# A two-layer trunk in float32 on one core: idle products in TensorE's waits, narrow spreads at the recurrence's end, the query norm multiplied into the queries

## The reference, cut to what matters

```python
def rwkv7_time_mix(...):
    ...
    y = wkv7_scan(r_h, heads(decay), k_h, v_h, -kk, kk * heads(a))
    mean = jnp.mean(y, axis=-1, keepdims=True)
    var = jnp.mean(jnp.square(y - mean), axis=-1, keepdims=True)
    y = ((y - mean) * lax.rsqrt(var + RWKV_GN_EPS)).reshape(B, T, C) * ln_w + ln_b
    bonus = jnp.sum(r_h * k_h * r_k, axis=-1, keepdims=True) * v_h
    y = (y + bonus.reshape(B, T, C)) * g
    return y @ w_out, v_raw

def nsa_mix(x, w_in, ...):
    q = rms_norm(proj[..., :NSA_Q_COLS].reshape(B, T, HKV, G, DH), q_norm)
    ...
    s = jnp.einsum('bqhgd,bnhd->bhgqn', qb, k_cmp) * scale - slopes * dist_c
    p_c = masked_softmax(s, dist_c >= 0)
    ...
    s = jnp.einsum('bqhgd,bhqkd->bhgqk', qb, k_sel) * scale - slopes * dist_s
    p_s = masked_softmax(s, dist_s >= 0)
    ...
    o = gb[..., 0:1] * o_c + gb[..., 1:2] * o_s + gb[..., 2:3] * o_w
```

## Time and profile before

| what | us |
|---|---|
| median of 3 runs | 800.62 (800.15 to 806.32) |
| the profiled execution, device time | 797.37 |
| its span, first to last instruction | 795.6 |
| TensorE busy | 744.3 (94%) |
| VectorE busy | 524.5 (66%) |
| ScalarE busy | 384.1 (48%) |
| GpSimd busy | 73.8 (9%) |
| mean granted clock of TensorE | 0.962 |

### The profile page before, as it was taken

One profiled execution on the slowest core, in us unless ns is written; L12 is line 12 of the kernel. 1 busy time (PEld: TensorE's weight loads), 2 busy tenths in 40 slices (PEclk: granted clock), 3 DMA queues, 4 the chain that ended last, 5 costly groups with the idle time before them and its releaser, 6 DMA issues.

```text
span 795.6 us, 18364 instructions
## 1 busy us (share of the span) xinstructions
PE 744.3 (94%) x7720; PEld 698.8 (88%) x7720; DVE 524.5 (66%) x751; ACT 384.1 (48%) x581; POOL 73.8 (9%) x67
## 2 busy tenths in 40 slices
PE   7999997797878999999999998988889999999997
PEld 6988987797747999999999988975569999999997
DVE  3996886757543887875555776676746887764541
ACT  6666543221433544544444443748867454444331
POOL 0000005280130000000000010023320000000000
PEclk9999998999977999999999999988989999999999
DMA  9953330000111599876666544300007566575651
GB/s 290 271 179 109 107 106 2 4 3 7 51 54 54 159 241 245 220 210 213 194 199 187 162 138 122 117 21 2 1 13 227 176 195 206 166 235 190 197 169 53
DMA packets 110893, 109.29 MB, mean 137 GB/s; under 512 B 7120, under 2 KB 109776, under 8 KB 110704
## 3 DMA queue, kind: packets, MB, share of 16 engines
q1 hardware_dynamic: 110832, 108.41, 45.5%
HBM read 107.35 MB, written 1.05 MB: 136 GB/s over the span
## 4 chain that ended last, share of the span: by engine, by line
PE 80%; DVE 10%; ACT 3%; SPq 2%; DMA 1%; issue 1%; POOL 1%; ACTq 0%; DVEq 0%; POOLq 0%
PE ps L449 21%; PE ps L450 20%; PE ps L451 20%; PE ps L664 4%; DVE SB L1972 2%; DMA raw<-in_rwkv_w_in 1%; DVE nmx L1977 1%; ACT SB L1405 1%; DVE Gs L1653 1%; PE ps L958 1%; PE ps L802 1%; PE ps L947 1%; PE ps L563 1%; PE ps L892 1%; DVE wlo L1468 1%
## 5 line engine op out<-in xcount | busy, mean ns | idle before, releaser
L1468 DVE TENSOR_TENSOR wlo<-raw,whi 128x1024 fp32r<-128x1024 f32 x188 | 225.3, 1221 | 88.5 <-ACT whi L1069 86.0
L449 PE MATMUL ps<-xh,whi 128*128 128x256 f32 x896 | 250.9, 280 | 0.5 <-DVE wlo L1468 0.5
L450 PE MATMUL ps<-xl,whi 128*128 128x256 f32 x896 | 247.9, 277 | 0.0
L451 PE MATMUL ps<-xh,wlo 128*128 128x256 f32 x896 | 247.8, 277 | 0.0
L1069 ACT ACTIVATE whi<-raw 128x1024 fp32r<-128x1024 f32 x124 | 130.1, 1058 | 129.2 <-PE ps L451 123.0
L449 PEld LDWEIGHTS ps<-xh,whi 128*128 128x128 f32 x896 | 168.3, 188 | 4.1 <-issue 2.5
L450 PEld LDWEIGHTS ps<-xl,whi 128*128 128x128 f32 x896 | 168.4, 188 | 0.3 <-issue 0.2
L451 PEld LDWEIGHTS ps<-xh,wlo 128*128 128x128 f32 x896 | 168.3, 188 | 0.0
L451 PE MATMUL ps<-hh,wlo 128*128 128x256 f32 x512 | 141.3, 276 | 0.0
L449 PE MATMUL ps<-hh,whi 128*128 128x256 f32 x512 | 141.3, 276 | 0.0
L450 PE MATMUL ps<-hl,whi 128*128 128x256 f32 x512 | 141.3, 276 | 0.0
(11 more groups left out here) (286 smaller groups left out, 1001.3 us busy)
## 6 DMA issues: line engine op xcount, KB each, us to landing
raw<-in_mlp_w SPq DMA_DIRECT2D x128, 512.0 KB, 4.4
raw<-in_rwkv_w_in SPq DMA_DIRECT2D x24, 512.0 KB, 4.9
raw<-in_nsa_w_in SPq DMA_DIRECT2D x20, 512.0 KB, 4.6
raw<-in_rwkv_w_out SPq DMA_DIRECT2D x8, 512.0 KB, 3.5
raw<-in_nsa_w_out SPq DMA_DIRECT2D x8, 512.0 KB, 3.9
cw<-in_nsa_cmp_w SPq DMA_DIRECT2D x4, 512.0 KB, 10.0
cst<-in_consts SPq DMA_DIRECT2D x1, 1047.0 KB, 11.1
xtok<-in_x SPq DMA_DIRECT2D x2, 512.0 KB, 4.6
```

Source lines behind the costliest of these rows:

```text
L449: mm(o, wh, hi[:, kk, :], start=(kk == 0), stop=False)
L450: mm(o, wh, lo[:, kk, :], start=False, stop=False)
L451: last = mm(o, wl, hi[:, kk, :], start=False, stop=(kk == ktiles - 1))
L1468: v.tensor_tensor(wlo[:, slot, :], raw[:, slot, :], whi[:, slot, :].bitcast(f32), ALU.subtract)\
```

## The change

In the inversion four products of `ident` with `chunk` (128x256) go into the PSUM bank of `sq1` before the wait for VectorE, for each stream and pair, and five before the waits in front of `g_products`; nobody reads them. In the recurrence `rsb` is gone: `gn_spread` multiplies the 16 x 64 reciprocals by eight slices of `spread`, one for each 128 features. Gate, bonus and lower part of the last two chunks are on VectorE, with the last chunk's gate multiplied into `YC` before the spread is there; GpSimd does the first two. Idle products (1, 2 and 5) stand in TensorE's queue between the last steps. In the attention the negated reciprocal norm is transposed, copied, spread to 128 features per tile and multiplied into the queries of groups 1 to 3 (`spread_q`, `scale_q`); in these groups slopes are constants, the scale of the exponential is -1 and the third instruction of `soft` is gone. Group 0 stays. Compressed scores, their exponential and gates move by one item, and `ahead(U0["vv"])` moves behind the last `out_lower`.

```diff
                                   start=True, stop=True)
                 last.then_inc(sem(f"inv_pe{s}"), 1)
+            def idle_products(bank, count):
+                for n in range(count):
+                    mm(ps[:, bank, 0:T], cc("ident"), cc("chunk"), start=True, stop=True)
...
                         pe.wait_ge(sem("bkt_dve"), 3)
                     lower_products(s, pair)
                 for s in both:
+                    idle_products(inv_bank(s, pair, "sq1"), 4)
                     dve_did(s, 3)
                     times(s, pair, "sq1", LT, 0)
                 for s in both:
...
                     times(s, pair, "m64b", LT, 0)
+            idle_products(inv_bank(0, NPAIR - 1, "m64a"), 5)
             for s in range(2):
                 pe.wait_ge(sem(f"inv_dve{s}"), NDVE * NPAIR)
             g_products(0)
...
             def gn_spread(c):
                 pe.wait_ge(sem("y_rstd"), c + 1)
-                mm(ps[:, 7, :], spread[0:H, D + FT:], rsb[:, :, :], start=True, stop=True).then_inc(sem("rstd_pe"), 1)
+                for k in range(FT):
+                    last = mm(ps[:, 7, k * C:(k + 1) * C], hspread(k), rst[:, 0:C], start=True, stop=True)
+                last.then_inc(sem("rstd_pe"), 1)
...
                     xs_values(c + 1)
                 if c:
                     gn_spread(c - 1)
+            def keep_warm(count):
+                for n in range(count):
+                    mm(ps[:, 4, 0:T], cc("ident"), cc("chunk"), start=True, stop=True)
             gn_mean(NCH - 1)
+            keep_warm(1)
             gn_var(NCH - 1)
+            keep_warm(2)
             gn_spread(NCH - 1)
+            keep_warm(5)
             pe.wait_ge(sem("yh_ready"), NCH)
-            pe.wait_ge(sem("yl_ready"), NCH - 1)
-            pe.wait_ge(sem("yl_last"), 1)
+            pe.wait_ge(sem("yl_ready"), NCH)
             linear8("o0", yh, yl)
             def mlp_pe(n1, n2, hi, lo, x, i_norm):
...
                               cc("hsel")[:, H - 2:H], start=True, stop=True)
             last.then_inc(sem("nsa_pe"), 1)
             scores(0)
+            pe.wait_ge(sem("nrq_ready"), 1)
+            for q in range(TT):
+                last = nc.tensor.transpose(ps[0:H, 4, q * P:(q + 1) * P], nrq[:, q, :], cc("ident"))
+            last.then_inc(sem("nsa_pe"), 1)
             values(1)
-            pe.wait_ge(sem("q_root"), 1)
+            def spread_q(j):
+                pe.wait_ge(sem("rqT_ready"), 1)
+                if j == 3:
+                    pe.wait_ge(sem("q_scaled"), 1)
+                for k in range(2):
+                    last = mm(ps[:, 7 - 3 * (j == 2), k * T:(k + 1) * T], hspread(2 * j + k), rqT[:, :], start=True, stop=True)
+                last.then_inc(sem("q_spread"), 1)
+            spread_q(1)
             scores(1)
             scores(2)
+            spread_q(2)
+            spread_q(3)
             pe.wait_ge(sem("kcm_r"), 2)
             pe.wait_ge(sem("vblk_r"), 4)
+            pe.wait_ge(sem("q_scaled"), 3)
             for q in range(TT):
                 for k in range(FT):
                     o = q * T + k * 32
...
                 A(rst[:, C:2 * C], ps[0:H, 7, 0:C], ACT.Sqrt, bias=tiny[0:H, 1:2], scale=1.0 / HD).then_inc(sem("y_std"), 1)
             def gn_upper(c):
-                if c < NCH - 1:
+                if c < NCH - 2:
                     act.wait_ge(sem("y_gated"), 2 * c + 2)
                 else:
-                    act.wait_ge(sem("y_last"), 2)
+                    act.wait_ge(sem("y_last"), 2 * (c - NCH + 2) + 2)
...
             act.wait_ge(sem("nsa_pe"), NSA_PE["q_sum"])
             A(nq[:, :, :], ps[:, 3, 0:TT * H].rearrange("p (q h) -> p q h", h=H), ACT.Sqrt, bias=tiny[:, 3:4])\
                 .then_inc(sem("q_root"), 1)
+            act.wait_ge(sem("nsa_pe"), NSA_PE["rq_T"])
+            A(rqT[:, :], ps[0:H, 4, 0:T], ACT.Copy, scale=-1.0).then_inc(sem("rqT_ready"), 1)
             ahead(U0["vv"])
...
                 act.wait_ge(sem("mx_ready"), n + 1)
                 for i in range(4):
                     hd = 4 * j + i
-                    o = A(SB[n % 4][:, i, 0:w], SB[n % 4][:, i, 0:w], ACT.Exp, bias=nmx[:, n % 4, i:i + 1], scale=nrq[:, q, hd:hd + 1],
+                    o = A(SB[n % 4][:, i, 0:w], SB[n % 4][:, i, 0:w], ACT.Exp, bias=nmx[:, n % 4, i:i + 1], scale=nrq[:, q, hd:hd + 1] if j == 0 else -1.0,
                           accum_out=den[:, q, b, hd:hd + 1])
                     step(o)
...
                     values(0)
                 if n == 3:
                     values(1)
-                if n == 1:
+                if n == 2:
                     act.wait_ge(sem("csub"), 1)
                     A(Sc[:, :, :, 0:16], Sc[:, :, :, 0:16], ACT.Exp).then_inc(sem("cexp"), 1)
...
             def gn_rstd(c):
                 dve.wait_ge(sem("y_std"), c + 1)
-                step(v.reciprocal(rst[:, 0:C], rst[:, C:2 * C]))
-                settle()
-                v.tensor_tensor(rsb[:, :, :], rst[:, 0:C].unsqueeze(1).broadcast_to([H, FT, C]),
-                                spread[0:H, D:D + FT].unsqueeze(2).broadcast_to([H, FT, C]), ALU.mult).then_inc(sem("y_rstd"), 1)
+                v.reciprocal(rst[:, 0:C], rst[:, C:2 * C]).then_inc(sem("y_rstd"), 1)
             def gn_scale(c):
...
                 if c:
                     gn_rstd(c - 1)
                 ahead(U0["v"] + 4 + c)
+            def late(c):
+                return YF[c % 2][:, :, :], slice(c * C, (c + 1) * C)
+            def late_lower(c):
+                y, tok = late(c)
+                dve.wait_ge(sem("yh_ready"), c + 1)
+                v.tensor_tensor(yl[:, :, tok], y, yh[:, :, tok].bitcast(f32), ALU.subtract).then_inc(sem("yl_ready"), 1)
             gn_scale(NCH - 2)
-            gn_rstd(NCH - 1)
-            gn_scale(NCH - 1)
-            tok = slice((NCH - 1) * C, T)
-            y = YF[(NCH - 1) % 2][:, :, :]
             dve.wait_ge(sem("gate_folded"), 3)
-            dve.wait_ge(sem("y_scaled"), NCH)
+            y, tok = late(NCH - 2)
+            dve.wait_ge(sem("y_scaled"), NCH - 1)
             v.tensor_tensor(y, y, Gt[:, :, tok], ALU.mult).then_inc(sem("y_last"), 1)
             dve.wait_ge(sem("y_last"), 1)
             v.tensor_tensor(y, y, t11[:, :, tok], ALU.add).then_inc(sem("y_last"), 1)
-            dve.wait_ge(sem("yh_ready"), NCH)
-            v.tensor_tensor(yl[:, :, tok], y, yh[:, :, tok].bitcast(f32), ALU.subtract).then_inc(sem("yl_last"), 1)
+            y, tok = late(NCH - 1)
+            dve.wait_ge(sem("yc"), NCH)
+            dve.wait_ge(sem("yh_ready"), NCH - 2)
+            dve.wait_ge(sem("yl_ready"), NCH - 2)
+            v.tensor_tensor(y, YC[:, :, :], Gt[:, :, tok], ALU.mult).then_inc(sem("yc_gated"), 1)
+            late_lower(NCH - 2)
+            gn_rstd(NCH - 1)
+            dve.wait_ge(sem("rstd_pe"), NCH)
+            dve.wait_ge(sem("yc_gated"), 1)
+            v.tensor_tensor(y, y, ps[:, 7, :].rearrange("p (k n) -> p k n", n=C), ALU.mult).then_inc(sem("y_last"), 1)
+            dve.wait_ge(sem("y_last"), 3)
+            v.tensor_tensor(y, y, t11[:, :, tok], ALU.add).then_inc(sem("y_last"), 1)
+            late_lower(NCH - 1)
             def residual(name, i, gain, x):
...
                 v.scalar_tensor_tensor(kcm[q, :, e, 0:NB], view(ps[q, 5, 0:HKV * 16]), tiny[q, 4:5],
                                        view(gu[q, 1, :]), ALU.mult, ALU.mult).then_inc(sem("kcm_r"), 1)
             dve.wait_ge(sem("q_root"), 1)
-            dve.wait_ge(sem("zeroed"), 7 + H)
-            step(v.tensor_tensor(qsl[:, :, :], nq[:, :, :], slp[:, :].unsqueeze(1).broadcast_to([P, TT, H]), ALU.mult))
-            step(v.tensor_scalar(nq[:, :, :], nq[:, :, :], -1.0, None, ALU.mult))
+            step(v.tensor_scalar(nrq[:, :, :], nq[:, :, :], -1.0, None, ALU.mult))
             settle()
-            step(v.reciprocal(nrq[:, :, :], nq[:, :, :]))
+            v.reciprocal(nrq[:, :, :], nrq[:, :, :]).then_inc(sem("nrq_ready"), 1)
+            dve.wait_ge(sem("zeroed"), 7 + 4)
+            step(v.tensor_tensor(qsl[:, :, :], nq[:, :, 0:4], slp[:, :].unsqueeze(1).broadcast_to([P, TT, 4]), ALU.mult))
             settle()
+            dve.wait_ge(sem("nrq_ready"), 1)
+            def scale_q(j):
+                x = Qn[:, 2 * j:2 * j + 2, :]
+                dve.wait_ge(sem("q_spread"), j)
+                v.tensor_tensor(x, x, ps[:, 7 - 3 * (j == 2), :].rearrange("p (k n) -> p k n", n=T), ALU.mult)\
+                    .then_inc(sem("q_scaled"), 1)
             gv = gat[:, :, :].rearrange("p q (h b) -> p q h b", b=3)
...
             def compressed_scores():
                 dve.wait_ge(sem("nsa_pe"), NSA_PE["sc"])
-                step(v.tensor_tensor(Sc[:, :, :, 0:NB], ps[:, 5, :].rearrange("p (q h n) -> p q h n", q=TT, n=16)[:, :, :, 0:NB],
-                                     nrq[:, :, :].unsqueeze(3).broadcast_to([P, TT, H, NB]), ALU.mult))
+                raw_ = ps[:, 5, :].rearrange("p (q h n) -> p q h n", q=TT, n=16)
```

(21 more changed lines are left out.)

## The result

The median of the changed kernel is 791.75 us (20 executions, 787.63 to 806.44), that of before 798.8 us (20 executions, 796.56 to 809.19). The ratio is 0.9897 with a 95% interval of 0.9872 to 0.9921: about 7 to 8 us less. The forecast was 0.9925 of before and 794.6 us, with a range of 788.5 to 801.0; the time lies in the range and the forecast's ratio just outside the interval, on the side of the smaller gain. The sum came out nearly right, but from terms of which two were wrong by 3 and 4 us, in opposite directions.

What follows compares the result with a forecast made beforehand. The prediction saw TensorE losing time and clock to waits in the inversion, recurrence end and attention. Terms of -1.9, -5.4 and +1.3 us summed to -6.0 us, forecasting 794.6 us, range 788.5 to 801 us.

Steps and rivals of the forecast that it cites:

- Inversion, -1.9 us: Inversion: idle products hold the clock, gaining 3.0 us; the five ahead of `g_products` delay the masks by 1.1 us.
- Rival 1: Inversion and recurrence tail: idle products don't hold the clock, so the kernel slows to 811.5 us; chance 5%.
- Narrow spread, 1.95 us: Recurrence's `gn_spread`: eight 64-column products, 16 records, take 1.95 us in place of one 512-column product of 1.1 us.
- Rivals 3 (0.5 us) and 5 (2.6 us): Group-norm spreads: cheap at 0.5 us each, 788.8 us total, 12%; or loads don't hide, 2.6 us each, 797.2 us, 5%.
- Up to the last mean, -1.5 us: Recurrence before the last mean: +0.2 us twice, and -1.9 us in the item with long `rsb`, where the clock holds.
- Tail, -1.8 us: Recurrence's end, from item 2's scaling to the projection: 10.3 us instead of 12.1, with one VectorE product fewer.
- Clock at `o0`, -2.1 us: Output projection's start: TensorE kept occupied through the tail, so the 2.1 us lost at half clock are gained.
- Into the steady loop, -1.6 us: Attention's start: compressed scores 4 us later, absorbed by TensorE's slack further on; 1.6 us gained into the loop.
- rival 2: Attention: the 4 us delay is not absorbed because ScalarE's first items are late too; +3.8 us there, 797.1 us; 20%.
- Steady loop, -0.9 us: Softmax loop: dropping the third VectorE instruction saves 0.9 us over three groups; immediate operands cost the same.
- The late `ahead`, +2.5 us: Attention loop's end: the last projection waits for `ahead(U0["vv"])`, 1.22 us, behind the last `out_lower`; 2.5 us lost.
- The clock at `o1`, +1.3 us: Last projection's start: 2.2 us of TensorE idling may drop the clock, costing 0 to 2.1 us; 1.3 taken.

Runs made afterwards that it cites:

- no_four: Changed kernel without the four idle products ahead of each first square of the inversion; 797.67 us, one execution.
- best1: Changed kernel without the five idle products, with `ahead(U0["vv"])` back behind softmax item 0 and four idle products ahead of the compressed scores; 789.57 us, 0.9871 of before.
- wide_spread: Changed kernel with the old single wide group-norm product and `rsb` instead of eight narrow products; 792.53 us, 0.9903 of before.
- p_inv: Original kernel with only the inversion's idle products added; 797.19 us, 0.9968 of before.
- p_att: Original kernel with only the attention changed; 798.03 us, 1.0009 of before.
- sc_idle: Changed kernel plus four idle products in the wait ahead of the compressed scores; 788.35 us, 0.9850 of before, five executions.
- no_warm: Changed kernel without the eight idle products at the recurrence's end; 797.62 us, 0.9970 of before.
- no_rec: Changed kernel with the recurrence and its end as in the original; 795.84 us, 0.9953 of before.
- p_inv_rec: Original kernel with the inversion and recurrence changed, attention as before; 800.85 us, 0.9982 of before.
- best1_no_warm: The kernel best1 without the eight idle products at the recurrence's end; 793.31 us, 0.9931 of before.

## Why the prediction came out right, point by point

- **Inversion, -1.9 us: right in every part.** 9.55 us for the 320 records (forecast 9.8), -3.4 us by no_four (-3.0), +1.4 by best1 (+1.1), -2.0 in all. Rival 1, that idle products don't hold the clock, is out.
- **Narrow spread, 1.95 us: right**, 1.99, and 1.92 from its start to that of the next product (234.42 to 236.34). Rivals 3 (0.5 us) and 5 (2.6 us) are out: 16 records, each with its own load on the same 16 rows, start 0.12 us apart. The rule of the Trainium skill that spoke against the spread ("TensorE: Matmul & The Clock Gate", Part 3) would have given 2.6 us by the forecast's estimate; the measurement decides for the overlap.
- **Up to the last mean, -1.5 us: too much.** Measured -0.4, and 0.4 to 0.9 us between kernels with like falls. The step "what follows keeps its clock, another 0.9 us" failed: in after the stretch from 220 to 225 us is at 0.78 and the last mean is at half clock, and its last mean takes 2.05 us with or without `rsb` (wide_spread). The long `rsb` was not what let the clock fall: p_inv and p_att have it and no fall near 220 us, best1 and sc_idle are without it and have one there.
- **Tail, -1.8 us: the sum nearly right (-1.4), one reason missing.** The product saved on VectorE was rightly credited: from the spread's end to `o0` it is 2.94 us instead of 3.85, the larger part of the gain. But the idle products, which I had counted only for the clock at `o0`, carry the tail as well: without them it takes 12.20 us in this form (no_warm), 0.9 more than before's. The terms that the forecast lists for the new tail add up to 8.6 us, and to 9.3 with the scaling ahead of the mean, not to its 10.3; the last 1.0 us is given no source.
- **Clock at `o0`, -2.1 us: right**, about -2.5.
- **Into the steady loop, -1.6 us: wrong, it was +1.6.** The start of the scores was forecast at 521.4 on the old scale, 4.1 us later relative to the query sums; measured 14.49 against 10.29 us, 4.2 later. The term that failed is the next one: I took the clock for unchanged by the new wait of 1.04 us. It was at half through the scores, 7.00 us instead of 3.96, and ate the slack that should have absorbed the delay: the transposes come 33.3 us behind the query sums (535.32 in the lines above) where before had 30.3, though the forecast had them a little earlier. With the clock held (sc_idle) the same delay was absorbed, 38.22 us to item 3 against before's 41.44. The outcome at this place is that of rival 2, but its cause, ScalarE's late first items, is not what the profiles show, and its total for the attention (+3.8 us) did not come.
- **Steady loop, -0.9 us: mis-sized, it was -5.2.** The three groups' worth of the third VectorE instruction is 3 x 0.36 = 1.1 us, near the 0.9. "The immediate operands are the same instructions and cost the same" was false: 3 x 0.96 = 2.9 us. The remaining 1.2 us go with the clock in items 4 to 7, as shown above; why it fell there before and not in after is open. The kind of operand is a mechanism that none of my rivals had; the trace of before has no such instruction with an immediate, and I gave the term no bounds.
- **The late `ahead`, +2.5 us: right**, +2.35, by the wait of 2.11 us that was forecast, on `wlo`. **The clock at `o1`, +1.3 us: 0 in after's profile**, where it stayed at full, but 1.4 us or more in four of the eight profiles with this wait. Between these two the forecast had chosen, and which it is changes with the execution.
- **The sum.** -6.0 forecast; the local terms give -2.0 -0.4 -1.4 -2.5 -1.3 = -7.6 us, the medians -7.05, the lowest runs -8.9. An error of 3.2 us against the change at the loop's start and one of 4.3 in its favour within the loop met in the sum, and so did 1.1 against it ahead of the last mean and 1.3 in its favour at `o1`; that the time fell into the forecast's range was in this part luck. The chances were less well placed than the range: 791.75 us lies under 792.6, for which the forecast had 0.28 against 0.67 for what lies above it up to 808.6.

**What stays open.** What decides the pace. It sets in at breaks of the stream and holds for 30 to 210 us. Behind `o0` the profiles of before, p_att, no_warm and no_rec are without it up to the query sums, the others have it for some stretch; at `o1` only after and no_rec have it. The medians of p_inv_rec, no_warm and wide_spread lie 6 to 9 us above their lowest runs, those of p_inv and p_att 2 to 3 us, which speaks for the recurrence's edit making it more frequent; but after, with that edit, has 4 us, no_rec, without it, 5, and before itself 1.6 to 3.8. Neither the narrow spreads (wide_spread) nor the idle products (no_warm) are its cause alone. More was not tried.

## What to carry to other kernels

Where TensorE waits a microsecond or two in a chain of small products, idle products that fit inside the wait are a cheap gain: here 3.4 us in the inversion and some 5 us at the recurrence's end (best1_no_warm against best1). Count each against the wait that it lies in, for five that did not fit cost 1.4 us. And when a factor is moved elsewhere, look at what kind of operand remains: an immediate in place of a per-partition column was worth more here than the instruction that the move took away, while a new wait of 1 us ahead of the compressed scores cost some 3 us through the clock. Look at the clock behind each wait in more than one execution, for in the same code it fell in some and held in others.

## What the runs showed of the hardware that I had not expected

- **Two paces at full clock.** Products of 128x256 in an unbroken stream start 0.113 or 0.118 us apart (179 or 172 in 20 us), both at a granted clock of 1.0. The same stretch from `o1` to the end took 203.6 to 205.6 us in twelve profiles and 211.3 in two. It makes single executions of one kernel differ by more than the whole change.
- **Column against immediate.** VectorE's scalar_tensor_tensor over 128x256: 477 against 415 ns, over 128x128: 342 against 282. ScalarE's exponential over 128x256 with a scale: 594 against 497 ns.
- **Sixteen rows of weights at half clock.** The sixteen records of a narrow spread take 1.99 us at full and 3.67 us at half clock; the one wide product 1.12 and 2.07.
